# The remainder of the turned expert rows, formed by GpSimd in place of VectorE

## The reference

```python
logits = (hf @ w_router + b_router).astype(jnp.float32)
top_vals, top_idx = lax.top_k(logits, TOP_K)
gates = jax.nn.softmax(top_vals, axis=-1).astype(h.dtype)
...
def expert_block(args):
    xb, e = args
    gu = xb @ w_gate_up[e] + b_gate_up[e]
    gate, up = gu[:, :D_EXPERT], gu[:, D_EXPERT:]
    gate = jnp.minimum(gate, SWIGLU_LIMIT)
    up = jnp.clip(up, -SWIGLU_LIMIT, SWIGLU_LIMIT)
    act = (up + 1) * (gate * jax.nn.sigmoid(SWIGLU_ALPHA * gate))
    return act @ w_down[e] + b_down[e]
```

## Time and profile before

| | |
|---|---|
| median of 3 runs | 1644.77 us (1643.59 to 1647.08) |
| the profiled execution, its own time | 1645.22 us |
| its span, first to last instruction | 1643.4 us |
| TensorE's mean granted clock | 0.992 of full speed |
| busy over the span: PE, PEld | 1606.8 us (98%), 1317.5 us (80%) |
| busy: DVE, ACT, POOL | 1342.1 us (82%), 1051.9 us (64%), 446.2 us (27%) |
| DMA | 485.82 MB, mean 296 GB/s; in the expert stage about 370 to 397 GB/s in nearly every slice |

### The profile page before, as it was taken

How to read it: one execution, slowest core, us unless ns; L and a number is a source line. 1 busy time by engine, 2 the same in 40 slices (tenths; PEclk the granted TensorE clock), 3 DMA queues, 4 the chain that set the end, 5 groups by cost and what they waited for, 6 DMA issues and landing times.

```text
span 1643.4 us, 24161 instructions
## 1 busy us (share of the span) xinstructions
PE 1606.8 (98%) x7853; PEld 1317.5 (80%) x7853; DVE 1342.1 (82%) x1050; ACT 1051.9 (64%) x912; POOL 446.2 (27%) x288
## 2 busy tenths in 40 slices
PE   8999999999998999999999999999999999999997
PEld 6797777788896778878888888888888888877885
DVE  6974555523658889999999999999999999999996
ACT  5533444422346667877777777777787777777774
POOL 0000000501104563354332233322342223333230
PEclk9999999999999999999999999999999999999999
DMA  7331222333358999999999999999999999999994
GB/s 245 117 103 52 77 77 77 120 98 104 132 198 309 361 343 366 385 379 393 395 393 373 391 397 393 392 374 392 396 394 389 373 384 395 386 388 374 371 377 164
DMA packets 117354, 485.82 MB, mean 296 GB/s; under 512 B 14973, under 2 KB 58217, under 8 KB 68023
## 3 DMA queue, kind: packets, MB, share of 16 engines
q1 hardware_dynamic: 104612, 456.59, 71.7%
q0 software_dynamic: 12704, 28.71, 7.5%
HBM read 469.78 MB, written 24.36 MB: 301 GB/s over the span
## 4 chain that ended last, share of the span: by engine, by line
PE 82%; DVE 7%; issue 4%; DMA 3%; ACT 2%; POOL 1%; DVEq 0%; POOLq 0%; ACTq 0%; SPq 0%
PE ps L657 26%; PE ps L658 25%; PE ps L659 25%; DVE w_lo L1347 2%; DMA more_raw<-in_w_down 2%; PE ps L897 2%; DVE work L1471 2%; DVE zT L1347 1%; PE ps L766 1%; PE ps L786 1%; DVE work L1647 1%; PE ps L775 1%; ACT w_hi L1020 1%; PE ps L926 1%; DMA r<-expert_inputs_by_quarter,quarter_at 0%
## 5 line engine op out<-in xcount | busy, mean ns | idle before, releaser
L1347 DVE TENSOR_TENSOR zT<-raw,zT 128x2048 fp32r<-128x2048 f32 x96 | 217.2, 2290 | 45.5 <-ACT zT L1020 42.1
L1785 POOL DMA_INDIRECT r<-expert_inputs_by_quarter,quarter_at x124 | 221.4, 1785 | 53.2 <-issue 28.7
L1347 DVE TENSOR_TENSOR w_lo<-more_raw,w_hi 128x2048 fp32r<-128x2048 f32 x96 | 217.3, 2291 | 9.1 <-ACT w_hi L1020 8.2
L1347 DVE TENSOR_TENSOR zT<-more_raw,zT 128x2048 fp32r<-128x2048 f32 x96 | 219.1, 2283 | 1.1 <-ACT zT L1020 1.1
L1020 ACT ACTIVATE w_hi<-raw 128x2048 fp32r<-128x2048 f32 x96 | 184.3, 1920 | 52.2 <-PE ps L659 36.2
L1347 DVE TENSOR_TENSOR w_lo<-raw,w_hi 128x2048 fp32r<-128x2048 f32 x96 | 215.7, 2272 | 2.4 <-issue 2.2
L657 PE MATMUL ps<-w_hi,xT 128*128 128x512 f32 x512 | 202.4, 395 | 8.7 <-DVE w_lo L1347 4.9
L1020 ACT ACTIVATE zT<-more_raw 128x2048 fp32r<-128x2048 f32 x96 | 184.3, 1920 | 36.4 <-PE ps L659 25.7
L657 PE MATMUL ps<-zT,xT 128*128 128x512 f32 x512 | 202.8, 396 | 0.6 <-DVE zT L1347 0.6
L659 PE MATMUL ps<-w_hi,xT 128*128 128x512 f32 x512 | 200.6, 392 | 0.0
L658 PE MATMUL ps<-w_lo,xT 128*128 128x512 f32 x512 | 200.5, 392 | 0.0
(11 more groups left out here) (276 smaller groups left out, 3167.0 us busy)
## 6 DMA issues: line engine op xcount, KB each, us to landing
more_raw<-in_w_gate_up SPq DMA_DIRECT2D x129, 1024.0 KB
raw<-in_w_gate_up SPq DMA_DIRECT2D x127, 1024.0 KB
raw<-in_w_down SPq DMA_DIRECT2D x65, 1024.0 KB
more_raw<-in_w_down SPq DMA_DIRECT2D x63, 1024.0 KB
raw<-in_w_in SPq DMA_DIRECT2D x29, 1024.0 KB, 5.4
r<-in_x SPq DMA_DIRECT2D x8, 512.0 KB, 6.2
raw<-in_w_branch_conv SPq DMA_DIRECT2D x4, 1024.0 KB, 5.3
raw<-in_w_out SPq DMA_DIRECT2D x4, 1024.0 KB, 4.9
```

Source lines behind the costliest of these rows:

```text
L1347: nc.vector.tensor_tensor(expert_pair(1, c), chunk, expert_pair(0, c).bitcast(F32), ALU.subtract).then_inc(split_lo, 2)
L1785: nc.gpsimd.indirect_dma_start(out=quarters[:, part, :], out_offset=None, in_=h2_quarters, in_offset=bass.IndirectOffsetOnAxis(ap=quarter_ ...
```

## The change

`rest_of_rows` is taken out of VectorE's `turn_block` and given to GpSimd, with the same tiles and the same operation (128 x 1024, float32 minus rounded float32, written in the rounded type). On GpSimd it stands between `gather_next` and `scatter` in each round; in the first round, which gathers later, it comes first. After the loop it runs once more. The sign `rows_lo` for TensorE and for `turn_rows` is now raised by GpSimd.

```diff
@@ VectorE
-            def rest_of_rows(g):
-
-                ve.wait_ge(rows_hi, g - 1)
-                nc.vector.tensor_tensor(xTl, rows_raw.rearrange("p (k n) -> p k n", n=P), xTh.bitcast(F32),
-                                        ALU.subtract).then_inc(rows_lo, 1)
-
-            ve.sem_inc(rows_lo, 1)
...
-                rest_of_rows(g + 1)
                 split_expert(g + 1, 0)
                 split_expert(g + 1, 1)
@@ GpSimd
+            gp.sem_inc(rows_lo, 1)
+
+            def rest_of_rows(before):
+
+                gp.wait_ge(rows_hi, before)
+                nc.gpsimd.tensor_tensor(xTl, rows_raw.rearrange("p (k n) -> p k n", n=P), xTh.bitcast(F32),
+                                        ALU.subtract).then_inc(rows_lo, 1)
+
...
                 g = before + 1
                 if not first:
                     gather_next(g)
+                rest_of_rows(before)
                 scatter(g, 2 * before, 2 * before + 2)
...
             with gp.Fori(1 + OVER_STEPS, but_one) as before:
                 turn_round(before)
+            rest_of_rows(but_one)
             scatter(nblk, 2 * but_one, 2 * nblk)
```

## The result

The changed kernel takes 1696.68 us (median of 4 runs, 1693.68 to 1699.46) against 1645.6 us before (4 runs, 1643.59 to 1647.08): a ratio of 1.0297, 95% interval 1.028 to 1.0315. Slower was forecast; 1654.5 us was not, and 1696.7 lies outside the range given. The span of the profiled execution grew from 1643.4 to 1697.6 us, by 54.2.

The account below looks back on a forecast made before the run. TensorE was taken to set the pace in clean rounds (34.36 us), VectorE right behind. Terms of 5.0, 2.9 and 1.6 us made 9.5, moving the span from 1643.4 to 1652.9 us; forecast 1654.5 us, range 1644 to 1675.

Parts of the forecast that it names:

- first rival: VectorE really is relieved: GpSimd holds it for less than the 1.14 us given back; 1639 us, chance 0.06.
- its own sign of being wrong: Prediction wrong if chunk 0's subtraction still takes 2.3 us, or takes 4.2 while rounds stay at 34.36 us.
- What it adds on GpSimd: The moved subtraction on GpSimd, taken as 2.15 us from a 96x1024 one; floor 1.22, upper bound 3.18 us.
- the sum: Added time: 5.0 us in 11 clean rounds, 2.9 in 19 other periods, 1.6 at first and last round; together 9.5.
- which closes a loop that TensorE has no part in: VectorE chunk 2 to chunk 0, GpSimd's copy, ScalarE's store and chunk 2: 34.76 us a round against 34.36.
- chunk 4 has 0.1 us of room: Small ScalarE waits further on, once the block head slips, were to make the 34.76 us round 34.8.
- second rival: Delay absorbed: GpSimd's copy precedes chunk 0, a late head gives VectorE time back; about 3 us, 1647 us, chance 0.14.
- of its 2.15 us, 0.15 lie before that: GpSimd's subtraction, 0.15 us of it before 1026.16, ends at 1028.16; chunk 0 then ends 0.79 us later.
- The prediction's other estimate, 2.25 us: GpSimd's subtraction as half the skill's 4497 ns at 2048 elements: 0.1 us more a round, some 3 us in total.
- Between 0 and 0.45 I take 0.15: Delay for each of the 19 other periods, set by arriving weights and single disturbances: 0.15 us each, 2.9 us.
- 0.45 for the clean rounds: Added time in each of 11 clean rounds, where TensorE alone set 34.36 us: 0.45 us each, 5.0 us.

Follow-up runs that it names:

- run 4: Kernel before with the `rest_of_rows` subtraction left out on every engine, signs raised as before (a measure, not usable): 1636.36 us, ratio 0.9933.
- run 1: Changed kernel with the first sign of `rows_lo` raised at the top of GpSimd's list: 1675.28 us, ratio 1.0173.
- run 2: Kernel before with only the first sign of `rows_lo` moved to GpSimd, subtraction still on VectorE: 1666.82 us, ratio 1.0119.
- run 6: Kernel before plus an extra GpSimd memset of a 128x1024 tile, which only writes: 1646.4 us, ratio 1.0003.
- run 7: Kernel before plus an extra GpSimd copy that reads one 128x1024 float32 tile: 1667.27 us, ratio 1.0126.
- run 8: Changed kernel with the first sign early and the subtraction split, 512 columns on GpSimd and 512 on VectorE: 1659.93 us, ratio 1.008.
- run 3: Kernel of run 1 with GpSimd's copy into `uix` ahead of its subtraction: 1675.43 us.
- run 5: Kernel before, VectorE's subtraction kept, plus an extra GpSimd subtraction of two 128x1024 float32 tiles that nobody waits for: 1730.81 us, ratio 1.0525.
- run 11: Kernel before with VectorE's second activation product (L1652 of half 1) behind chunk 0 instead of ahead of it: 1637.63 us, ratio 0.9933.

## Why the prediction was wrong

**What was right.** The direction, and the kind of loss: GpSimd's reads stop VectorE, VectorE loses more than it is given back, and TensorE waits at the head of its block. The first rival (VectorE really is relieved) fell, and run 4 gives its bound, 1636 us; the forecast for it was 1639.

**What was not: the place of the stop and the path behind it.** The prediction let the stop fall on chunk 0, which was to take 4.2 us, and named as its own sign of being wrong that chunk 0 still takes 2.3. It takes 2.28. The stop fell on L1652 instead. The copy was to last near 2 us and the store to wait for `uix`: the copy lasts 0.67 us, and in the steady rounds the store waits for TensorE. The steady rounds are 35.53 us, not 34.8.

**The missing step: the first sign of `rows_lo`.** "What it adds on GpSimd" prices one instruction. The change moves two, and the second is the increment without which TensorE may not start block 1. In the kernel before GpSimd issues its last record at 556.97 us, while TensorE was in block 1 from about 538 us. Nothing in the sum or the rivals stands for it. It cost 20 to 23 us (runs 1 and 2), more than a third of the 51.1, where the sum had nothing.

**"which closes a loop that TensorE has no part in" named the wrong loop.** The copy into `uix` did not meet chunk 0: it ended at 1033.25, with L1652, 1.4 us before the store. The loop that sets the round does go through TensorE: end of chunk 0, head of the block, L897, ScalarE's turned activations, ScalarE's chunk 4, VectorE from chunk 4 to chunk 0. The prediction mentions it in passing ("chunk 4 has 0.1 us of room"), and the second rival argues that a late head gives VectorE its time back. It does not, since chunk 4 moves with the head. In numbers of the trace after: from the end of chunk 0 (1035.41) to chunk 4 (1044.74) 9.33 us; from there to the end of the next chunk 0 (1068.70 + 2.28 = 1070.98) 26.24; sum 35.57. Before, in the round of the earlier trace rows, chunk 4 and the next instruction behind it were:

```profile
1004.59 4.49 DVE L1347 TENSOR_TENSOR w_lo<-more_raw,w_hi 128x2048 fp32r<-128x2048 f32 x2
```

The second part was then 1029.51 - 1004.59 = 24.92; with 9.33 that makes 34.25, only 0.11 below TensorE's 34.36. The trace of before has both parts in one round, where TensorE waits for chunk 0: from the end of chunk 0 (1339.99) to chunk 4 (1349.28) 9.29 us, from there to the end of the next chunk 0 (1374.88) 25.60, of which 0.60 is a wait for chunk 7, whose weights came late. Without it this makes 34.29. Everything that is put between chunk 4 and chunk 0 beyond 0.11 us should then lengthen the round one for one, and six runs say so:

| run | stop of L1652 | VectorE's own work | 34.25 + both | round measured |
|---|---|---|---|---|
| 6, write only | 0 | 0 | 34.25 | 34.36 (TensorE) |
| 7, one tile read | 1.07 | 0 | 35.32 | 35.27 |
| 8, halves | 1.36 | -0.54 | 35.07 | 35.05 |
| the change | 2.44 | -1.14 | 35.55 | 35.53 |
| 3, copy first | 2.57 | -1.14 | 35.68 | 35.65 |
| 5, extra subtraction | 2.44 | 0 | 36.69 | 36.7, alternating with 38.3 |

**"of its 2.15 us, 0.15 lie before that" was mis-sized.** GpSimd's subtraction takes 2.41 us on 128x1024 elements, and it stopped VectorE for 2.44, not 1.93. The output type is not the reason: run 5, all float32, has 2.40 and 2.44. It was also not L1652 that went first, as the step assumed. The prediction's other estimate, 2.25 us, is short as well.

**"Between 0 and 0.45 I take 0.15" for the other periods was too little.** The loop is a floor under every steady round: from 804.84 us on all 24 have 35.53 us, the later ones too, which had 34.9 on average before (L1672 at 1185.21 and, twelve rounds on, at 1603.64). For those it is 0.66 us each, not 0.15. Nor is 0.45 for the clean rounds enough: each has 1.17 us more. Runs 4 and 11 add that the later rounds had no slack of their own: the same small room at the head of the block had let late weights through to the round.

By the starts of L1672 (before 562.57, 772.89 and 1603.64; after 584.41, 804.84 and 1657.49) the 54.2 us of the two spans fall into 21.8 ahead of the first round (the sign), 10.1 in the first six rounds, 21.9 in the following 24, and 0.4 at the end. The sum had 0.8, 0.9 (six at 0.15), 6.9 (eleven at 0.45 and thirteen at 0.15) and 0.8 for these. Six rounds at the floor of 35.53 would be 2.9 us more than the six before; what goes beyond it lies in two long rounds, the second (38.79 us, 35.52 before) and the fifth (40.48, 36.07 before). In the fifth the path that the prediction priced is there for once. GpSimd was still in `over_step` until 732.4 us and through its gathers only at 744.7. VectorE and GpSimd there, and the waits from 728.8 to 769.3 us:

```profile
743.73 2.28 DVE L1347 TENSOR_TENSOR w_lo<-raw,w_hi 128x2048 fp32r<-128x2048 f32 x1
744.72 3.50 POOL L1879 TENSOR_TENSOR xT<-r,xT 128x1024 fp32r<-128x1024 f32 x1
```

```profile
ACT r L1241 <- POOL uix L1865: 6.7, 1, 6.7
PE ps L657 <- POOL xT L1879: 3.3, 1, 3.3
```

TensorE waits for the subtraction itself (the granted clock behind that wait is 0.50, from 748.0 to 751.5 us) and the store for `uix`, 6.7 us where it was 5.6 in this round before. In run 3, where the copy stands first, no store waits for `uix` in the first rounds, and this round takes 35.68 us. The second round, with a late gather ahead of it, was not taken apart.

**What stays open.** L1652 starts 0.16 us before GpSimd's subtraction (1030.08 and 1030.24) and still waits for all of it; in run 3 the lead is 0.31 us (1004.04 against 1004.35). In the fifth round of the change chunk 1 leads by 0.99 us (rows above); it keeps its 2.28 us, and GpSimd's subtraction ends 2.21 us behind it. A small copy that started 0.16 us behind L1652 waited for it in the earlier trace rows, and did not in run 3 (0.20 us). The one case with a long lead thus went the other way, but what decides between the two engines at 0.2 to 0.3 us wasn't settled. The earlier trace rows also have a GpSimd instruction with one tile as input that left a VectorE subtraction at its 1.23 us, while the one of run 7 stopped L1652; why is open. In the later rounds of the kernel before weights come late (0.60 us in the round taken apart above), and 0.6 us of room at the head of the block is enough to make these waits vanish; why they begin only after a dozen clean rounds is open too.

## What to carry to other kernels

Before work is moved to GpSimd to relieve VectorE, count the time for which GpSimd reads SBUF (the on-chip memory that both work in) as VectorE's time, if VectorE's instructions at that moment have two inputs there: here 2.44 us of stopping were paid for 1.14 us of relief. When a step moves to another engine, look for its first, free-standing signal and for what stands in front of it in the new list. And on an engine with no room, what counts is the order ahead of the one result that the bottleneck waits for next: putting a 0.6 us instruction behind it brought the 10 us that the move was after.

## What the runs showed of the hardware that was not expected

- GpSimd's reads stop L1652, a VectorE instruction with two SBUF inputs, and GpSimd's writes don't: 0.97 us of writing cost it nothing, a copy that reads one tile 1.07 us, a subtraction that reads two 2.44 us, one of half the length 1.36 us. No semaphore stands behind these stops, though the section on the chip says that engines wait for one another only through semaphores; and the profile counts them as busy time.
- The Trainium skill, SBUF — State Buffer (Who interferes with whom), says the same of an instruction that only writes; run 6 agrees. It also says that the order of issue decides which of the two is blocked. By the start times in the trace that did not hold for L1652, with a lead of 0.16 to 0.31 us, and did for a VectorE instruction with a lead of 0.99 us.
- In run 5 a wait of 2.0 us on TensorE, in a stage where it was otherwise busy without a gap, was followed in about every other round by a granted clock of 0.55 (near the lower of the two levels, 1.2 GHz) for 3.4 us. In the rounds between, a wait of 2.02 us was followed by a clock of 1.00, and so were the waits of 0.85 us in the change, where the matmuls go on at 0.23 to 0.24 us a step. The length of the wait alone does not decide.
